# The rotary-key transpose of a page step, issued half a step earlier on VectorE

## The reference, cut to what matters

```python
def _decompress(c_kv, w_ukv, g_kn):
    kv = jnp.einsum('btc,chd->bthd', c_kv, w_ukv)
    return _rmsnorm(kv[..., :NOPE], g_kn), kv[..., NOPE:]

def _attn_partial(qn, qp, kn, kp, v, mask):
    s = (jnp.einsum('bqhd,bkhd->bhqk', qn, kn) + jnp.einsum('bqhr,bkr->bhqk', qp, kp)).astype(jnp.float32) * SCALE
    ...
    m = jnp.max(s, axis=-1)
    e = jnp.exp(s - m[..., None])
    return m, jnp.sum(e, axis=-1), jnp.einsum('bhqk,bkhd->bhqd', e, v.astype(jnp.float32))

def _sample_attention(qn, qp, kn_new, kp_new, v_new, cache_ckv, cache_kpe, layer, page_table, w_ukv, g_kn):
    ...
    def step(carry, phys):
        c_blk = cache_ckv[layer, phys]
        kp_blk = cache_kpe[layer, phys]
        kn_blk, v_blk = _decompress(c_blk, w_ukv, g_kn)
        return _merge(carry, _attn_partial(qn, qp, kn_blk, kp_blk, v_blk, None)), None

    carry, _ = lax.scan(step, init, page_table.T)
```

## Time and profile before

| | |
|---|---|
| median of 3 runs | 1288.2 us (1286.38 to 1288.36) |
| the profiled execution's own time | 1280.55 us |
| its span, first to last instruction | 1278.6 us |
| mean granted TensorE clock | 0.987 |
| TensorE busy | 1207.4 us, 94% of the span |
| VectorE busy | 766.2 us, 60% |
| ScalarE busy | 419.6 us, 33% |
| GpSimd busy | 212.9 us, 17% |

### The profile page before, as it was taken

The page is one execution under the profiler, slowest core; times in us unless marked ns, Lnnn a source line. Parts: engine busy times, 40 slices in busy tenths (PEclk is TensorE's granted clock), DMA queues, the critical chain, the costliest instruction groups (busy, mean ns, idle before and its releaser), DMA issues. The chain is left out here.

```text
span 1278.6 us, 23966 instructions
## 1 busy us (share of the span) xinstructions
PE 1207.4 (94%) x8907; PEld 675.3 (53%) x8907; DVE 766.2 (60%) x1928; ACT 419.6 (33%) x1008; POOL 212.9 (17%) x246
## 2 busy tenths in 40 slices
PE   6999999989999999999989979999999999989898
PEld 3545677745665565654444445555444444454343
DVE  4000437957686877757868877887766667430331
ACT  3000354323333334332534333334344344210310
POOL 0000134711021212146313320000100100000000
PEclk9999999999999999989999989999999999989999
DMA  6413112123232322522532233422455333101000
GB/s 218 168 55 87 35 33 67 55 56 92 68 90 59 86 72 76 114 72 62 168 95 76 74 97 120 155 60 64 135 141 157 92 94 86 38 0 37 17 21 33
DMA packets 176117, 106.33 MB, mean 83 GB/s; under 512 B 119249, under 2 KB 168849, under 8 KB 175874
## 3 DMA queue, kind: packets, MB, share of 16 engines
q1 hardware_dynamic: 171666, 94.72, 26.3%
q10 hardware_dynamic: 2288, 5.89, 1.4%
q0 software_dynamic: 2048, 4.20, 1.4%
HBM read 75.78 MB, written 4.07 MB: 62 GB/s over the span
## 5 line engine op out<-in xcount | busy, mean ns | idle before, releaser
L552 PE MATMUL PS<-wk,c_T 128*128 128x512 f32 x1024 | 494.3, 608 | 7.9 <-DVE c_T L663 7.0
L552 PEld LDWEIGHTS PS<-wk,c_T 128*128 128x128 f32 x1024 | 178.6, 194 | 180.7 <-issue 150.6
L682 DVE TENSOR_REDUCE ssq<-PS 128x8 f32<-128x512 f32 x256 | 175.9, 687 | 156.5 <-ACT PS L598 153.6
L598 ACT ACTIVATE PS<-PS 128x512 f32<-128x512 f32 x256 | 150.5, 588 | 321.1 <-PE PS L552 320.4
L483 POOL DMA_INDIRECT r_ring<-in_cache_kpe,group_rows x64 | 62.1, 970 | 337.6 <-DVE r_T L671 329.9
L1555 PE MATMUL PS<-xnT,w_ring 128*128 128x276 f32 x416 | 101.0, 400 | 0.0
L1393 PE MATMUL PS<-w_ring,xnT 128*128 128x424 f32 x256 | 96.6, 535 | 0.9 <-DVE xnT L1042 0.9
L1555 PEld LDWEIGHTS PS<-xnT,w_ring 128*128 128x128 f32 x416 | 77.8, 190 | 20.6 <-issue 4.1
L1393 PEld LDWEIGHTS PS<-w_ring,xnT 128*128 128x128 f32 x256 | 48.8, 194 | 45.5 <-issue 45.4
L663 DVE STREAM_TRANSPOSE c_T<-blocks 128x512 f32<-128x512 f32 x95 | 66.2, 697 | 0.0
L2789 PE MATMUL PS<-w_g,nT 128*128 128x512 f32 x128 | 56.1, 595 | 0.0
(11 more groups left out here) (534 smaller groups left out, 1827.3 us busy)
## 6 DMA issues: line engine op xcount, KB each, us to landing
c_ring<-in_cache_ckv SPq DMA_DIRECT2D x256, 128.0 KB, 2.1
blocks<-c_ring SPq DMA_DIRECT2D x380, 64.0 KB
w_ring<-in_w_in SPq DMA_DIRECT2D x4, 1696.0 KB, 12.3
w_ring<-in_w_in SPq DMA_DIRECT2D x9, 512.0 KB, 5.1
w_o<-in_w_out SPq DMA_DIRECT2D x8, 512.0 KB, 4.4
w_g<-in_w_ple_gate SPq DMA_DIRECT2D x8, 512.0 KB
xn<-in_x_prompt SPq DMA_DIRECT2D x4, 512.0 KB, 11.1
w_ring<-in_w_in SPq DMA_DIRECT2D x2, 1024.0 KB, 6.1
```

The source lines that it names most:

```text
L552: mm = pe.matmul(PS[:, NORM[v % 2], :], c_T[:, u % 2, k, t * P:(t + 1) * P], wk[:, k], start=(k == 0), stop=(k == 1))
L598: nc.scalar.activation(PS[:, NORM[v % 2], :], PS[:, NORM[v % 2], :], ACT.Square).then_inc(no_sb, 1)
L682: dve.tensor_reduce(ssq[:, u % 2, t * H:(t + 1) * H], PS[:, NORM[v % 2], :].rearrange("p (h c) -> p h c", h=H), AX.X, ALU.add).then_inc(re ...
```

## The change

`turned_r(u+1)`, which stood in slot (u+1, 0) between `turned_blocks(u+1, 1)` and `scales(u)`, now stands at the end of slot (u, 1), behind `reduce(u, 1)`. The first one, `turned_r(0)`, moves from slot (0, 0) into the slot before the first step, between `turned_c(0)` and a memset. No instruction is added or dropped, and the orders of the other engines stay as they were.

```diff
             yield
             turned_c(0)
+            turned_r(0)
             dve.memset(c_ring[:, :, :, KVL:KVL + 1], 1.0)
             yield
             for u, t in slots:
@@
                 if t == 0:
                     if u >= 1:
                         turned_blocks(u, 1)
-                    turned_r(u)
                     if u >= 1:
                         scales(u - 1)
@@
                         turned_blocks(u + 1, 0)
                 reduce(u, t)
+                if t == 1 and ahead:
+                    turned_r(u + 1)
                 yield
```

## The result

The changed kernel took 1291.02 us, the median of 16 runs (1287.66 to 1297.85). The kernel before took 1288.22 us beside it (16 runs). The ratio is 1.0033, with a 95% interval from 1.002 to 1.0045: slower by 0.33%, or 2.6 to 5.8 us. The prediction was 1285.9 us with 1289.6 as its upper end, so it was wrong in sign and outside its range.

A forecast was written before the change was run, and what follows sets the result against it. TensorE, busy 94% of the span, was taken to set the pace. Tail -4.2, prompt attention +1.5 and earlier stages +0.4 gave -2.3 us, from 1288.2 to 1285.9 us, with an 8-in-10 range of 1282.6 to 1289.6.

The forecast's parts named there:

- The queues that the step moves past: GpSimd's gathers, released earlier: lateness for a transpose and the first step's wait counted at nothing, at most 0.5 us.
- Rival C: Tail and attention: the gather beside `score` makes the inserted L671 dearer, up to 23 us slower, 1311 us; chance 0.08.
- The tail: Steps 42 to 63: L515 released 0.19 us sooner, bound by L663's end; 22 x 0.19 = 4.2 us gained.
- The cover under L659: Tail: L659 ends 0.19 us later, but TensorE's 0.55 us ahead of L515 absorbs it, 0.17 us to spare.
- Rival B: Tail: `norms`, moved back by L659, hold L515 and hide the gain; 1290.1 us, or 1288.0 with half; chance 0.17.
- The prompt attention: VectorE's chain to `pr` has no pause, so each of 8 waits grows by 0.19 us; 1.5 us lost.
- The earlier stages on VectorE: Before the prompt attention: six places lose 0.19 us each, four waits on `r_T` gain 0.19; 0.4 us lost.
- The sum: Whole kernel: -4.2 + 1.5 + 0.4 = -2.3 us.
- The base of it all: One profiled execution, 1280.55 us; the runs' median was 0.6% above, and the forecast difference was carried over to it.
- The price of an insertion on VectorE: L671 in its new place costs its spacing to the next instruction, 0.19 us, not its whole 0.27.

The follow-up runs named there:

- early steps: Against the kernel before, only the transposes into `r_T` of steps 0 to 32 stand at the new place; 1292.24 us, ratio 1.005.
- tail alone: Against the kernel before, only the transposes into `r_T` of steps 42 to 63 stand at the new place; 1283.69 us, ratio 0.9983.
- attention alone: Against the kernel before, only the transposes into `r_T` of steps 33 to 41 stand at the new place; 1289.96 us, ratio 1.0028.
- the best: Changed kernel with the transpose ahead of the slot-1 sum, gathers released a step later, and L515's two waits exchanged; 1279.03 us, ratio 0.9931.

## Why the prediction was wrong

- **The queues that the step moves past: this step failed, and with it the sign.** I asked only whether a gather could be late for its transpose, and counted its earlier release at nothing. The question was what the release sets off: `r_T` of step 3 lets the gather of step 6 run behind three others, and so on. Its price, 2.3 to 3.4 us, is the growth of the wait for `pa`. The runs that delay the gathers alone show it: that wait is 2.1 to 2.4 us in four traces of the old order (none in the one that I read), 4.6 to 6.1 in five with the gathers released earlier, and 0.8 to 0.9 in three with them delayed. Rival C had the gather as a cause, but beside `score`; L704 kept its length (334 ns in the mean, 344 before).
- **The tail: mis-sized.** The mechanism held: the waits for `r_T` went, and the release moved to L663's end. L515 was to follow it by 0.05 us and took 0.15, since the wait that now ends last is an instruction of its own. 4.2 became 2.2 us. The cover under L659 was right: with only the order of the waits changed, the step is 9.23 us, with L659 as late as in the changed kernel. Rival B allowed for half of the gain, but for L659's sake; the 9.32 us without L659's delay and this 9.23 with it rule that out.
- **The prompt attention: right.** 1.6 us for 1.5, and 0.1 when the transpose stands ahead of the sum.
- **The earlier stages on VectorE: right as far as can be seen.** Of the groups that the first trace of the changed kernel and the second of before both have, L515's early waits fall by 0.6 us and L552's rise by 0.3; three smaller ones (L527, and two in stages) rise by 0.2 to 0.3 each, 0.7 together. That is 0.4 us lost in sum, as forecast. The 1.7 us for `spread`, which come up in three traces, of both orders, are left out.
- **The sum:** -2.2 + 1.6 + 0.4 + 2.3 to 3.4 = 2.1 to 3.2 us slower, against 2.8 by the medians and 2.6 to 5.8 by the ratio. Of the 4.4 to 5.5 us between the forecast of -2.3 and this sum, the gathers make 2.3 to 3.4 and the tail 2.0.
- **The base of it all.** I read one execution, in which the gathers hardly held TensorE up, so no row pointed at this price. That execution lay 7.7 us under the median. I noted the gap and took the difference over, instead of asking what the others had: longer waits, and a lower clock (below).
- **The price of an insertion on VectorE: right.** 8 insertions cost 1.6 us, 0.20 each. The section of the Trainium skill that the prediction sets against this price (VectorE: DVE Perf Modes, The DRAIN you can't avoid) adds that a next instruction that is not held starts earlier, so the trace need not disagree with it.

**The granted clock beside the waits.** Each timed run has TensorE's mean granted clock on record, and within one kernel the runs with a lower clock are longer as a rule. Over the 219 runs with a clock on record, one slope fitted to all kernels, each with a level of its own, gives 0.95 us for each 0.001 of clock (an estimate). The kernel before has 0.984 in the mean of each of its three sets, the changed one 0.981 and 0.983. Put to one clock by this slope, the runs differ from the kernel before of their set (for the first set of the changed kernel, from the mean of the three) by, in us, uncertain by about 1, the early steps by 1.4:

| | at one clock | by the waits and steps in the traces |
|---|---|---|
| tail alone | -2.6 | -2.2 |
| attention alone | +1.7 | +1.6 |
| early steps alone | +3.2 | +2.7 to +3.8 |
| the whole change | +2.0, again +2.3 | +2.1 to +3.2 |

So the early steps (1.005) and the attention (1.0028) read higher in their times than in their waits because their runs had a lower clock, and the loss of the change is not the clock's alone. The exchanged waits come to 2.6 us lost in the kernel before, 1.8 gained in the changed one and 1.9 in the best, for 2.0 expected. The clock also makes about half of the gap between the two executions of the kernel before: 0.987 against 0.982 is 4.7 us by the slope, and the waits for `pa` and `spread` are 4.1, of 8.9 us between the spans.

Left open: whether the earlier gathers themselves bring the lower clock of the changed kernel, or chance does. With the gathers delayed its runs had 0.983, and with the transpose ahead of the sum as well 0.982, and both were faster than the kernel before. At one clock they gain 4.3 and 5.7 us on it, more than the waits listed here give. Why the first execution of the kernel before was spared was not tried either.

## What to carry to other kernels

When an instruction is moved, follow what it releases on every queue, and ask there not only "does it come in time?" but "what does it now run back to back with?". Where an instruction waits for two semaphores, write first the one that will end last, and look again after a change that turns their order round. Before costing a change from one trace, look how that execution stands to the median, in its waits and its granted clock: a wait that is absent in a lucky one is still paid in the others.

## What the runs showed of the hardware

While GpSimd issues gathers, TensorE's semaphores can reach the other engines late, and several that are due are then seen together. In the changed kernel, three groups of matmuls that end at 293.37, 293.63 and 295.35 us are all seen at 296.69 to 296.79. Counted from the matmuls' ends, the copy into `pa` started 0.50 us late behind two gathers with a pause after them, 1.92 behind three in a row, 3.34 behind four; but 0.05 behind the same three in one execution of the kernel before. VectorE's and ScalarE's semaphores were not seen to be held in this way: in the same stretch of the changed kernel ScalarE's square is seen 0.01 us after its end (292.91), and so is VectorE's sum (293.64). The Trainium skill, Perfetto Trace Analysis, section Summary: the profiler window per engine type, says that a semaphore's way to the other engines is in no row of TensorE. The rows agree: L1711's row ends at 293.38, and the 3.34 us until the copy are in none. The ends of matmuls are modelled in these views, so the rows cannot tell a late semaphore from a late end of the matmul itself. How the gathers hold them was not found out.

A wait that stands as an instruction of its own costs 0.09 us more than one on the weight load itself, in both kernels: a tail step is 9.32 instead of 9.23 us in the changed one, 9.51 instead of 9.42 in the kernel before.
